# A gated-delta-net and transformer chain on one core: first head's decay moved ahead of v's silu, five output tiles held open through the last head, and the norm's sum issued one step later

## The reference

```
hn = rmsnorm(x)
q, k, v, gate, a, b = hn @ w_in        # per head i (8 heads): 128 channels each of k, q, v, gate
q, k, v = silu(causal_conv4(q, k, v))  # k and q are normalised
decay, beta from a, b                  # per token and head
# chunks of 128 tokens: T = inverse of (I + lower(beta * decay * k k^T)), u = T v, w = T k
# for each chunk c: v_new = u - w S;  o = q S + (q k^T * decay) v_new;  S = cd * S + k^T v_new
o = rmsnorm(o) * silu(gate)            # per head
h = x + concat(o) @ w_out              # 1024 x 1024
h = h + relu(rmsnorm(h) @ w1)^2 @ w2   # 4096 wide
```

## Time and profile before

| | us |
|---|---|
| median of three runs | 1432.51 (1431.48 to 1432.53) |
| the profiled execution, device time | 1432.37 |
| its span in the trace | 1430.6 |
| PE busy | 1391.6 |
| DVE busy | 751.1 |
| ACT busy | 592.3 |

### The profile page before, as it was taken

The page is one execution under the profiler, slowest core; times in us unless marked ns, Lnnn a source line. Parts: engine busy times, 40 slices in busy tenths (PEclk is TensorE's granted clock), DMA queues, the critical chain, the costliest instruction groups (busy, mean ns, idle before and its releaser), DMA issues.

```text
span 1430.6 us, 18545 instructions
## 1 busy us (share of the span) xinstructions
PE 1391.6 (97%) x6729; PEld 1140.2 (80%) x6729; DVE 751.1 (53%) x1112; ACT 592.3 (41%) x928; POOL 0.2 (0%) x4
## 2 busy tenths in 40 slices
PE   7799999999989999999999999999999999999998
PEld 5678888888768888888887777777888888888886
DVE  6577777777464334343456533447643443434555
ACT  5454454555344223142245545544442331323342
POOL 0000000000000000000000000000000000000000
PEclk9899999999999999999999999999999999999999
DMA  4221322311133333333333311121433232333323
GB/s 149 79 65 51 64 66 59 73 58 44 63 103 90 104 91 104 97 88 103 90 102 118 118 55 49 44 60 59 163 103 103 88 104 88 98 105 91 88 88 103
DMA packets 42338, 124.09 MB, mean 87 GB/s; under 512 B 3952, under 2 KB 12720, under 8 KB 41776
## 3 DMA queue, kind: packets, MB, share of 16 engines
q1 hardware_dynamic: 33472, 117.08, 27.3%
q10 hardware_dynamic: 8816, 6.33, 2.2%
HBM read 119.17 MB, written 4.23 MB: 86 GB/s over the span
## 4 chain that ended last, share of the span: by engine, by line
PE 94%; DVE 3%; ACT 2%; issue 1%; DMA 1%; SPq 0%; ACTq 0%; DVEq 0%
PE acc L306 26%; PE acc L308 25%; PE acc L307 25%; PE ps L421 2%; PE ps L443 2%; PE ps L643 2%; PE ps L627 1%; PE ps L659 1%; PE ps L401 1%; DVE wl L281 1%; DMA raw<-in_weights 1%; ACT wh L275 1%; PE ps L671 0%; PE ps L464 0%; PE ps L395 0%
## 5 line engine op out<-in xcount | busy, mean ns | idle before, releaser
L306 PE MATMUL acc<-xh,wh 128*128 128x512 f32 x1008 | 416.6, 413 | 10.6 <-DVE xl L1776 8.5
L308 PE MATMUL acc<-xh,wl 128*128 128x512 f32 x1008 | 395.5, 392 | 0.0
L307 PE MATMUL acc<-xl,wh 128*128 128x512 f32 x1008 | 394.6, 391 | 0.0
L281 DVE TENSOR_TENSOR wl<-raw,wh 128x1024 fp32r<-128x1024 f32 x208 | 253.7, 1220 | 70.4 <-ACT wh L275 67.3
L275 ACT ACTIVATE wh<-raw 128x1024 fp32r<-128x1024 f32 x208 | 217.2, 1049 | 173.8 <-DMA raw<-in_weights 154.6
L306 PE MATMUL acc<-yh,wh 128*128 128x512 f32 x624 | 244.4, 392 | 7.1 <-DVE h L1557 5.5
L308 PE MATMUL acc<-yh,wl 128*128 128x512 f32 x624 | 242.9, 389 | 0.0
L307 PE MATMUL acc<-yl,wh 128*128 128x512 f32 x624 | 242.8, 389 | 0.0
L306 PEld LDWEIGHTS acc<-xh,wh 128*128 128x128 f32 x1008 | 190.8, 189 | 50.3 <-DVE wl L281 8.7
L308 PEld LDWEIGHTS acc<-xh,wl 128*128 128x128 f32 x1008 | 190.2, 189 | 41.0
L307 PEld LDWEIGHTS acc<-xl,wh 128*128 128x128 f32 x1008 | 190.9, 189 | 37.6 <-issue 4.3
(11 more groups left out here) (233 smaller groups left out, 1173.9 us busy)
## 6 DMA issues: line engine op xcount, KB each, us to landing
raw<-in_weights SPq DMA_DIRECT2D x208, 512.0 KB, 3.5
work<-rows ACTq DMA_DIRECT2D x16, 256.0 KB, 7.1
h<-in_xT SPq DMA_DIRECT2D x4, 512.0 KB, 6.3
proj<-work ACTq DMA_DIRECT2D x2, 1024.0 KB, 4.1
work<-proj SPq DMA_DIRECT2D x2, 1024.0 KB, 7.4
outT<-h SPq DMA_DIRECT2D x8, 256.0 KB, 2.6
cst<-in_cst SPq DMA_DIRECT2D x1, 640.0 KB, 3.8
work<-in_pT SPq DMA_DIRECT2D x1, 512.0 KB, 6.0
```

The source lines that it names most:

```text
L281: nc.vector.tensor_tensor(wl[u.const % 4][:], raw[u.const % 2][:], wh[u.const % 4][:].bitcast(F32), ALU.subtract).then_inc(lo_done, 1)
L306: nc.tensor.matmul(dst[:], hi, mh[:, k, :], start=(n == 0), stop=False)
L307: nc.tensor.matmul(dst[:], hi, ml[:, k, :], start=False, stop=False)
L308: mm = nc.tensor.matmul(dst[:], lo, mh[:, k, :], start=False, stop=(n == KT - 1))
```

## The change

Three places are edited.

First head: on ACT the first tap of v and an explicit load of the Ln and Exp set stand ahead of the square of k, the decay follows, and v's silu comes last, with another load of the set behind it. On DVE the gate tile is taken right behind v's (unit 3; it used to be taken in head 1), one tap of v comes before the decay chain, and two taps come behind `Ti`.

All heads: `pe_norm` moves from behind x(2) to behind tx(2), with the unit steps between the two ahead of it.

Last head: five output units are held open, unit 36 with them. Units 34 to 37 lie in `ps[0]`, `ps[2]`, `ps[1]`, `ps[3]`; unit 36's split weights go into `xh[:, 6:8]` and `xl[:, 6:8]`, so they no longer wait for a slot. LAST_FILL grows from 28 to 35 steps (2 behind the last os becomes 3, 4 behind the norm becomes 10). ACT does the gate's silu and both loads of table sets ahead of unit 35's split, and splits unit 36 behind the squares of o. In the output phase DVE adds a tile to h first, then finishes the tile before it, and the splits ahead stand at one a tile.

```diff
+        def slot(u):
+            if u.per == 0 and u.const == U_OUT1 + 4:
+                return xh[:, 6:8, :].rearrange("p k t -> p (k t)"), xl[:, 6:8, :].rearrange("p k t -> p (k t)")
+            return wh[u.const % 4], wl[u.const % 4]
+        def slot_free(u):
+            return u.number({U_OUT1 + 4: -4, U_OUT1 + 8: -7}.get(u.const, -3) if u.per == 0 else -3)
...
-            if u.per == 0 and u.const in (U_OUT1 + 2, U_OUT1 + 3):
-                return ps[(u.const - U_OUT1 - 2) * 2]
+            if u.per == 0 and U_OUT1 + 2 <= u.const < U_OUT1 + 6:
+                return ps[(0, 2, 1, 3)[u.const - U_OUT1 - 2]]
...
-                beside = u.per == 0 and u.const in (U_OUT1 + 4, U_OUT1 + 5)
-                pe.wait_ge(evac[b], u.half(-1 if beside else 0))
+                beside = u.per == 0 and u.const in (U_OUT1 + 6, U_OUT1 + 7)
+                pe.wait_ge(evac[b], u.half(-2 if beside else 0))
...
             def x(n):
-                    if n == 2 and past:
-                        pe_norm(pe, b)
             def tx(n):
+                    if n == 2 and past:
+                        pe_norm(pe, b)
...
-        OUT_AHEAD = ((4, 5), (5,), (5,), (), (), (), (2,), (2,))
-        LAST_FILL = [1, 1, 0, 1, 1, 1, 1, 1, 1, 2, 2, 1, 1, 1, 1, 1, 1, 1, 1, 1, 1, 2, 4]
+        OUT_AHEAD = ((5,), (5,), (5,), (5,), (), (), (), (2,))
+        LAST_FILL = [1, 1, 0, 1, 1, 1, 1, 1, 1, 2, 2, 1, 1, 1, 1, 1, 1, 1, 1, 1, 1, 3, 10]
...
                 silu(qc, 6, q_silu)
+                first_tap(2)
+                act.preload_act_table_set(LN_EXP)
                 act_ksq(act, 0)
-                first_tap(2)
-                silu(vc, 9, v_silu)
-                act.preload_act_table_set(LN_EXP)
                 act_decay(act, 0)
                 nc.scalar.activation(eg, grow, ACT.Exp).then_inc(eg_d, 1)
                 act_knorm(act, 0)
+                silu(vc, 9, v_silu)
+                act.preload_act_table_set(LN_EXP)
...
             if past:
                 act_yh(act, b)
+            if not project:
+                act_gs(act, i)
+                act.preload_act_table_set(LN_EXP)
...
             nc.scalar.activation(osq, ps[5][:], ACT.Square).then_inc(osq_d, 1)
             if not project:
+                split_hi(act, Unit(U_OUT1 + 4))
                 act_onorm(act, i)
...
                 take(2)
-                for _ in v_taps:
-                    pass
+                take_gate()
+                next(v_taps)
                 next_knorm()
...
                 next_ti()
+                for _ in v_taps:
+                    pass
...
             upd(1)
-            take_gate()
+            if past:
+                take_gate()
...
             dve_osum(dve, H)
+            split_lo(dve, Unit(U_OUT1 + 4))
             dve_o1(dve, H)
...
+                dve_stream_add(dve, n, u)
+                if n > 0:
+                    dve_stream_norm(dve, n - 1, "mlp_g")
                 for ahead in OUT_AHEAD[n]:
                     split_lo(dve, u.plus(ahead))
-                dve_stream_tile(dve, n, u, "mlp_g")
+            dve_stream_norm(dve, KT - 1, "mlp_g")
```

More of the change, by code:

```diff
@@ L273, in split_hi @@
             if not u.known_below(4):
-                act.wait_ge(unit_done, u.number(-3))
-            nc.scalar.activation(wh[u.const % 4][:], raw[u.const % 2][:], ACT.Copy).then_inc(hi_done, 1)
+                act.wait_ge(unit_done, slot_free(u))
+            nc.scalar.activation(slot(u)[0][:], raw[u.const % 2][:], ACT.Copy).then_inc(hi_done, 1)
         def split_lo(dve, u):
@@ L279, in split_lo @@
             if not u.known_below(4):
-                dve.wait_ge(unit_done, u.number(-3))
-            nc.vector.tensor_tensor(wl[u.const % 4][:], raw[u.const % 2][:], wh[u.const % 4][:].bitcast(F32),
-                                    ALU.subtract).then_inc(lo_done, 1)
+                dve.wait_ge(unit_done, slot_free(u))
+            hi, lo = slot(u)
+            nc.vector.tensor_tensor(lo[:], raw[u.const % 2][:], hi[:].bitcast(F32), ALU.subtract).then_inc(lo_done, 1)
         def accumulator(u):
-            if u.per == 0 and u.const in (U_OUT1 + 2, U_OUT1 + 3):
-                return ps[(u.const - U_OUT1 - 2) * 2]
+            if u.per == 0 and U_OUT1 + 2 <= u.const < U_OUT1 + 6:
+                return ps[(0, 2, 1, 3)[u.const - U_OUT1 - 2]]
             return acc[u.const % 2]
         def unit_steps(pe, u, mh, ml, gate=None, order=range(KT), freed=None):
-            b, s, dst = u.const % 2, u.const % 4, accumulator(u)
+            b, (whi, wlo), dst = u.const % 2, slot(u), accumulator(u)
             pe.wait_ge(lo_done, u.number(1))
             if not u.known_below(2) and dst is acc[b]:
-                beside = u.per == 0 and u.const in (U_OUT1 + 4, U_OUT1 + 5)
-                pe.wait_ge(evac[b], u.half(-1 if beside else 0))
+                beside = u.per == 0 and u.const in (U_OUT1 + 6, U_OUT1 + 7)
+                pe.wait_ge(evac[b], u.half(-2 if beside else 0))
             for n, k in enumerate(order):
@@ L304, in unit_steps @@
                     gate(k)
-                hi, lo = ch(wh[s], k), ch(wl[s], k)
+                hi, lo = ch(whi, k), ch(wlo, k)
                 nc.tensor.matmul(dst[:], hi, mh[:, k, :], start=(n == 0), stop=False)
@@ L502, in build @@
         assert sum(FILL) == sum(FIRST_FILL) == 4 * KT
-        OUT_AHEAD = ((4, 5), (5,), (5,), (), (), (), (2,), (2,))
-        LAST_FILL = [1, 1, 0, 1, 1, 1, 1, 1, 1, 2, 2, 1, 1, 1, 1, 1, 1, 1, 1, 1, 1, 2, 4]
-        assert sum(LAST_FILL) == 4 * (KT - 1)
+        OUT_AHEAD = ((5,), (5,), (5,), (5,), (), (), (), (2,))
+        LAST_FILL = [1, 1, 0, 1, 1, 1, 1, 1, 1, 2, 2, 1, 1, 1, 1, 1, 1, 1, 1, 1, 1, 3, 10]
+        assert sum(LAST_FILL) == 5 * (KT - 1)
         def pe_out_steps(pe):
             pe.wait_ge(yl_d, H - 2)
-            units = [unit_steps(pe, Unit(U_OUT1 + n), yh, yl) for n in range(4)]
+            units = [unit_steps(pe, Unit(U_OUT1 + n), yh, yl) for n in range(5)]
             for unit in units[:2]:
@@ L518, in pe_out_steps @@
                 yield
+            pe.wait_ge(tt_d, H * 6)
             for unit in units[2:]:
-                pe.wait_ge(tt_d, H * 6)
+                if unit is units[4]:
+                    pe.wait_ge(nw_d, H)
                 for _ in range(KT - 1):
@@ L779, in _ @@
             next(out_steps)
-            for n in range(4, KT):
+            for n in range(5, KT):
                 run_unit(pe, Unit(U_OUT1 + n), yh, yl)
@@ L986, in act_gdn @@
                 first_tap(2)
-            act_gs(act, i)
+                act_gs(act, i)
             for c in range(1, C):
@@ L991, in act_gdn @@
                 silu(vc, 9, v_silu)
-            act.preload_act_table_set(LN_EXP)
-            if project:
+                act.preload_act_table_set(LN_EXP)
                 act_knorm(act, i)
@@ L1308, in take_gate @@
             def take_gate():
-                u = Unit(-1, i, 4)
+                u = Unit(-1, i, 4) if head else Unit(3)
                 dve.wait_ge(unit_done, u.number(1))
-                if past:
+                if head and past:
                     dve.wait_ge(g_silu, b)
@@ L1553, in dve_stream_tile, with dve_stream_add @@
         def dve_stream_tile(dve, m, u, gname):
+            dve_stream_add(dve, m, u)
+            if gname is not None:
+                dve_stream_norm(dve, m, gname)
+        def dve_stream_add(dve, m, u):
             b = u.const % 2
@@ L1557, in dve_stream_tile, with dve_stream_norm @@
             nc.vector.tensor_tensor(h[:, m, :], accumulator(u)[:], h[:, m, :], ALU.add).then_inc(evac[b], 1)
-            if gname is None:
-                return
+        def dve_stream_norm(dve, m, gname):
             n = tile_n[0]
```

## The result

The changed kernel took 1408.05 us (median of four runs, 1406.92 to 1408.48) against 1432.35 us before: the ratio is 0.983, 95% interval 0.9813 to 0.9847. That is 24.3 us faster; forecast were 21.1 us and 1411.4 us, with a range from 1409.0. The direction is right and each of the three parts gains, but more than forecast: the time lies 1 us under the range.

A forecast was written before the change was run, and what follows sets the result against it. PE, busy 1391.6 of 1430.6 us, was taken as the bound, so only its idle time counted. Gains of 5.9 + 8.2 + 7.0 = 21.1 us off 1432.37 gave 1411.3, predicted as 1411.4 us; range 1409.0 to 1415.5.

The forecast's parts named there:

- First head: First head into head 1: 5.9 us gained, 4.5 at unit 5 plus 1.4 of clock; bounds 2.7 and 6.2.
- Norm's sum: All heads: moving the sum behind tx(2) removes seven of PE's eight waits for DVE's addition, 8.2 us; bounds 4 and 8.2.
- Last head and output units: Last head and output phase: four PE waits, 7.6 us, go, less two costs of 0.3: 7.0 us; bounds 4.3 and 7.6.
- step (4): Output phase: separate banks end the 3.30 us wait before unit 38, not paid back because DVE is busy 59%.
- (2): Last head: ten steps behind the norm, 7.0 us, cover the 5.4 us chain to yl; the 1.52 us wait goes.
- (3): Output units: unit 36 no longer waits for slot or bank; unit 37's late split leaves 0.3 us idle.
- (5): Last head, a cost: silu and table loads ahead of unit 35's split delay ACT's tx(6) copy 0.4 us, PE 0.3.
- head 1 at the slow clock: Rival, chance 0.11: clock falls again in head 1 or unit 5's split is later; first head gives 2.7 to 4.5 us.
- a new wait in the loop: Rival, chance 0.05: in each head another DVE or ACT wait replaces the norm's; 4 us less, 1415.5 us.
- the tail at half: Rival, chance 0.05: DVE and ACT limit the output phase with add, norm and split a tile; 3 us less, 1414.4.
- a drain at table switches: Rival, chance 0.03: table switches at three places in the first and last heads cost a drain, 3.7 us, 1415.1.
- a late norm result: Rival, chance 0.02: norm's result reaches DVE too late, seven heads lose 3 us or more each; 1433 and above.

The follow-up runs named there:

- one alone: Changed kernel with a semaphore for each of the two table DMAs, so the decay waits for the first only: 1408.39 us, ratio 0.9822 to the kernel before.
- the other 0.8 us: Changed kernel with unit 5's high split put ahead of v's silu on ACT: 1407.19 us, ratio 0.9816 to the kernel before.
- both 3.3: Changed kernel with separate table-DMA semaphores and unit 5's high split ahead of v's silu: 1404.72 us, ratio 0.9798 to the kernel before.

## Why the prediction was off

**What bounds the kernel: right.** Only PE's idle time counted. ACT got two more table loads and DVE's work stayed the same, and neither shows in the total.

**First head: the mechanisms right, 5.9 forecast, 6.4 to 6.5 in the trace.** The decay waits for the second table DMA, as foreseen. I put its landing at 44.35, which is 43.1 on the changed trace's clock; it was 42.8, hence 3.0 instead of 2.7 at x(1). Unit 5's split took the gate tile's place. Unit 5 began 4.8 us sooner behind the landmark (60.77 - 22.04 against 54.66 - 20.75; forecast 4.5), and the other 1.6 are the clock's, where I had counted 1.4 of 1.7. The median of this part alone was 4.9 us faster: three of its five runs had a lower mean granted clock and took 1.7 us more than the traced one.

**Norm's sum: the mechanism right, the term mis-sized.** "The wait is gone and not replaced" holds in all seven heads. The step "8.8 - 0.56 = 8.2 us", with 8.2 as upper bound, failed: it priced a wait by the idle time the profile lists. It measured 10.1 us. Both of the lengths that I needed stood in the trace of before: x(2) starts at 144.47 and without the wait the next instruction would start 0.82 us later, while the norm's product starts at 146.72, 1.4 us after that. This term holds 1.9 of the 3.2 us by which the sum fell short, and it put the true time outside the range. Even my three upper bounds, 6.2 + 8.2 + 7.6 = 22.0, stay under the 24.3 measured.

**Last head and output units: 7.0 forecast, 7.7 measured, and the reason partly wrong.** Four lost overlaps of 0.16 us make up most of the difference. What was wrong is step (4), that banks of their own remove the 3.30 and that "it isn't paid back behind" because DVE is busy only 59% of the time. A share of busy time said nothing about a chain that goes between two engines: with the banks but the old order PE stops 4.5 us at the first MLP unit. DVE's new order, which I described and gave no price, is what keeps the gain. It alone is worth 4.7 of the 7.7. Of my steps (2), (3) and (5) the trace shows each: no wait for yl, 0.43 for unit 37 where I had 0.3, and 0.2 for ACT's copy where I had 0.3.

**The clock.** "An idle stretch of 3.3 us in otherwise busy work left the clock at 1.00" was a fact of one execution. Four other kernels here show it fall behind pauses of 1.9, 2.2, 3.3 and 4.5 us. I should have widened the range downwards for it, since all edits remove idle time.

**The rivals.** In the traced execution of the changed kernel, head 1 at the slow clock, a new wait in the loop, the tail at half, a drain at table switches, and a late norm result did not happen. That the first did not happen was luck in part: with the same head 1, the trace of DVE's old order shows the fall and 2.8 us lost, and one of five further runs of the changed kernel took 1411.52 us at a mean clock of 0.997. The rival "the tail gives only half" named the right mechanism (add, norm and split a tile); it comes true when DVE's order is put back.

## What to carry to other kernels

Price a wait of PE by the distance between the starts of the instructions around it, less their usual distance, not by the idle time listed: here each wait cost 0.16 to 0.25 us more than it showed. Before calling an engine free because it is half idle, follow one tile through its round trips to the other engines; issuing the next tile's first step ahead of the current tile's last ones was worth 5.7 us alone, the banks and the fifth open unit without it about 2 (an estimate, 8.1 - 6.0, across two chips). Where an edit only moves a chain forward, look what PE waits for next and what the granted clock does behind that wait, and test the two edits together: here one alone gave nothing, because the clock took its 1.5 us, the other 0.8 us, and both 3.3.

## What the runs showed of the hardware

The granted clock isn't a function of the length of the pause alone. Behind 3.3 us of idle time in the output phase it stayed up in two executions (1.00 over 40 us in the kernel before) and fell in a third (0.68 over 5 us). Behind 1.9 us of idle time, with another 1.4 and 0.2 us shortly before, it fell as well (0.62 over 4.5 us). A gain of 1.4 to 1.7 us can thus hang on removing a wait that is itself about as long. Ahead of x(1) of head 1 it fell behind an idle 2.78 us in the changed kernel (0.57 over 4 us) and stayed at 1.00 behind 2.6 us of the same wait in the kernel with DVE's old order. The start of the program differs from run to run as well: ahead of any edit, the first head's row-sum product came between 20.75 and 22.75 us in the profiled executions.
